# First attention of a two-layer trunk: the projections of the pair two ahead move from the turn's end to behind the next pair's transposes, and the raw values are kept in two places and copied by ScalarE

## The reference, cut to what matters

```python
def _mla_project(hn, pos, w_in, g_q, w_qup, g_kv, g_qn):
    ...
    q = (_rms_norm(c_q, g_q) @ w_qup).reshape(b, l, A_HEADS, A_DQK)
    q = _rms_norm(jnp.concatenate([q[..., :A_NOPE], _rope(q[..., A_NOPE:], pos)], axis=-1), g_qn)
    return q, _rms_norm(c_kv, g_kv), _rope(k_pe, pos)

def _mla_keys(latent, k_pe, w_kvup, g_kn):
    ...
    k = _rms_norm(jnp.concatenate([kv[..., :A_NOPE], k_pe_h], axis=-1), g_kn)
    return k, kv[..., A_NOPE:]
```

## Time and profile before

| what | us |
|---|---|
| median of 3 executions (lowest 2487.96, highest 2492.0) | 2488.02 |
| the profiled execution | 2487.95 |
| its span, first to last instruction | 2486.1 |
| TensorE busy in the span | 2292.0 (92%) |
| VectorE busy | 1729.8 (70%) |
| ScalarE busy | 1072.8 (43%) |
| GpSimd busy | 350.0 (14%) |
| the first attention's turns 0 to 5 | 521.52 to 767.79 |

### The profile page before, as it was taken

How to read it: one execution, slowest core, us unless ns; L and a number is a source line. 1 busy time by engine, 2 the same in 40 slices (tenths; PEclk the granted TensorE clock), 3 DMA queues, 4 the chain that set the end, 5 groups by cost and what they waited for, 6 DMA issues and landing times. The chain is left out here.

```text
span 2486.1 us, 45839 instructions
## 1 busy us (share of the span) xinstructions
PE 2292.0 (92%) x16594; PEld 2198.7 (88%) x16594; DVE 1729.8 (70%) x2714; ACT 1072.8 (43%) x1759; POOL 350.0 (14%) x300
## 2 busy tenths in 40 slices
PE   4999999588878989999999999999979989999997
PEld 4999999577877989999987899999867878999997
DVE  8976974456666599499535895795456657985973
ACT  5533532345555455145322552453236555542541
POOL 1000001134344100000114000001044321000001
PEclk9999999778988999999999999999978789999998
DMA  2222232000000222222213223223221212222221
GB/s 105 101 87 91 101 114 66 19 19 9 18 9 26 77 80 95 104 85 91 91 60 131 89 99 110 85 84 102 68 51 40 46 30 85 102 91 87 101 103 60
DMA packets 72794, 187.35 MB, mean 75 GB/s; under 512 B 40720, under 2 KB 42288, under 8 KB 61440
## 3 DMA queue, kind: packets, MB, share of 16 engines
q1 hardware_dynamic: 71424, 181.67, 21.7%
q0 software_dynamic: 1280, 4.49, 0.5%
HBM read 178.79 MB, written 7.35 MB: 75 GB/s over the span
## 5 line engine op out<-in xcount | busy, mean ns | idle before, releaser
L566 PE MATMUL ps<-xs_hi,w_hi 128*128 128x272 f32 x1408 | 411.6, 292 | 50.0 <-DVE w_lo_more L1515 28.3
L568 PE MATMUL ps<-xs_hi,w_lo 128*128 128x272 f32 x1408 | 409.4, 291 | 0.0
L567 PE MATMUL ps<-xs_lo,w_hi 128*128 128x272 f32 x1408 | 408.4, 290 | 0.0
L1038 ACT ACTIVATE w_hi<-raw 128x1408 fp32r<-128x1408 f32 (+3 forms) x124 | 145.9, 1183 | 507.1 <-PE ps L591 246.9
L1067 ACT ACTIVATE w_hi<-w_blocks 128x1024 fp32r<-128x1024 f32 x176 | 186.8, 1062 | 326.3 <-PE ps L568 160.5
L566 PEld LDWEIGHTS ps<-xs_hi,w_hi 128*128 128x128 f32 x1408 | 267.8, 190 | 53.9 <-issue 29.8
L566 PE MATMUL ps<-xs_hi,w_hi_more 128*128 128x272 f32 x1056 | 306.2, 290 | 1.2 <-ACT scratch L1113 0.9
L567 PE MATMUL ps<-xs_lo,w_hi_more 128*128 128x272 f32 x1056 | 305.7, 290 | 0.0
L591 PE MATMUL ps<-hid_hi,w_hi 128*128 128x272 f32 x1312 | 273.7, 290 | 9.1 <-DVE w_lo L1485 5.5
L591 PE MATMUL ps<-hid_hi,w_lo 128*128 128x272 f32 x1312 | 272.3, 289 | 0.0
L591 PE MATMUL ps<-hid_lo,w_hi 128*128 128x272 f32 x1312 | 272.3, 289 | 0.0
(11 more groups left out here) (249 smaller groups left out, 5259.7 us busy)
## 6 DMA issues: line engine op xcount, KB each, us to landing
w_blocks<-w_ffn_in SPq DMA_DIRECT2D x88, 1024.0 KB, 4.8
raw<-w_ffn_out SPq DMA_DIRECT2D x64, 704.0 KB, 4.1
raw<-w_b_kv SPq DMA_DIRECT2D x16, 512.0 KB, 3.6
raw<-w_a_out SPq DMA_DIRECT2D x8, 512.0 KB, 3.7
raw<-w_b_q SPq DMA_DIRECT2D x8, 512.0 KB, 3.6
raw<-w_b_out SPq DMA_DIRECT2D x8, 512.0 KB, 3.7
raw<-w_a_in SPq DMA_DIRECT2D x4, 672.0 KB, 4.0
raw<-w_a_qup SPq DMA_DIRECT2D x8, 288.0 KB, 2.8
```

What stands on the lines that cost most here:

```text
L566: pe.matmul(out, lhs[0], rhs[0], start=start, stop=False, skip_group_check=more)
L567: pe.matmul(out, lhs[0], rhs[1], start=False, stop=False, skip_group_check=more)
L568: return pe.matmul(out, lhs[1], rhs[0], start=False, stop=stop, skip_group_check=more)
L1038: act.activation(wh[par][:, 0:n], raw[par][:, 0:n], ACT.Copy).then_inc(w_hi, 1)
```

## The change

What it does, by engine:

- TensorE: `turn_staged` transposes the queries first, waiting for them alone ("qn"), then computes head 0's values (`between`), then waits for the keys and transposes them. `project_q` and `project_kv` of pair p + 2 come right behind, ahead of head 1's transposes; `w_uses` is reordered to match. Head 1's values now end the turn.
- ScalarE: the weight splits open the turn (in turn 6, `ahead`, the output projection's first unit). Behind the staging come `project(p + 2)`, which now copies both keys and raw values (L1307 of the changed kernel is the values' copy), and the squares of the keys.
- VectorE: the weight splits open the turn. Keys are normalised inside `stage`, behind the two query lows. `take_q` and `project` follow the staging; the five copies of raw values are gone. The sums of squares of the keys stand at the end of the turn, ahead of the output's low part.
- GpSimd: the queries of pair p + 2 between the two heads' normalisations, then the power for the keys, the staged values, the shared key part.
- The raw values of even pairs lie in the upper columns of `raw[0]` and `raw[1]` (`v_even`), those of odd pairs in `vr` (`v_odd`). The loop's body holds two turns, and runs three times. SP waits for GpSimd's staged values of pair 6 before it loads the output projection's units.

The arithmetic is the same. The core of the diff, first the tables, SP and TensorE:

```diff
 PROJ = {
     "pe": ["q0", "q1", "kv0", "kv1", "kv2", "kv3"],
-    "act": ["sqq", "k0", "k1", "k2", "k3", "k4", "sqk"],
...
+    "act": ["k0", "v0", "k1", "v1", "sqq", "k2", "v2", "k3", "v3", "k4", "v4", "sqk"],
+    "dve": ["q0", "q1", "q2", "rope_c", "rope_a", "rope_b", "rope", "ssq", "msq", "ssk", "ssk2", "ms", "kn"],
...
+        v_even = (raw[0][:, SLOT - 4 * 2 * DV:SLOT].rearrange("p (t g w) -> p t g w", t=4, g=2),
+                  raw[1][:, SLOT - NT * 2 * DV:SLOT].rearrange("p (t g w) -> p t g w", t=NT, g=2))
+        v_odd = (vrv[:, 0:4], vrv[:, 4:NK])
...
-            every += turned(1)
             if mla:
                 every += [(f"q{n}", p + 2, projects, [("proj", "dve", f"q{n}")]) for n in range(3)]
-                every += [(f"kv{n}", p + 2, projects, [("proj", "dve", f"v{n}")]) for n in range(5)]
+                every += [(f"kv{n}", p + 2, projects, [("proj", "act", f"v{n}")]) for n in range(5)]
+            every += turned(1)
...
+            sp.wait_ge(*M["stagev"]["pool"].at("v", PAIRS - 2))
             load_out(MO)
...
                     if mla:
-
-                        pe.wait_ge(*prj["pool"].at("kpe", it))
-                        pe.wait_ge(*prj["dve"].at("kn", it))
+                        pe.wait_ge(*prj["pool"].at("qn", it))
...
                     for name, v, t0 in (("tq", qsv, 0), ("tp", ksv, 0), ("tc", ksv, NT)):
+                        if mla and name == "tp":
+                            if between is not None:
+                                between()
+                            pe.wait_ge(*prj["pool"].at("kpe", it))
+                            pe.wait_ge(*prj["dve"].at("kn", it))
...
-                    if stages and not mla:
+                    if stages:
                         turn_staged(p + 1, uses, before, lambda: values(0, p))
                     else:
                         values(0, p)
-                        if stages:
-                            turn_staged(p + 1, uses, before)
+                    if mla and projects:
+                        project_q(p + 2, uses, before)
+                        project_kv(p + 2, uses, before)
...
                     values(1, p)
-                    if mla and projects:
-                        project_q(p + 2, uses, before)
-                        project_kv(p + 2, uses, before)
```

ScalarE:

```diff
-                def turn_of(p, stages, projects):
+                def turn_of(p, stages, projects, odd=False):
+                    if mla and projects:
+                        split_units(p + 2)
+                    elif mla and stages:
+                        ahead(U + 2 * PAIRS)
                     split_p(0, 0, p)
                     if not mla:
                         stage_values(p)
-                    elif stages:
-                        square_keys(p + 1)
...
                     if stages:
                         stage(p + 1)
-                        if mla and projects:
-                            split_units(p + 2)
-                        elif mla:
-
-                            ahead(U + 2 * PAIRS)
+                    if mla and projects:
+                        project(p + 2, odd)
+                        square_keys(p + 2)
```

VectorE:

```diff
+                        if mla and step == "q":
+                            norm_keys(it)
...
                 def turn_of(p, stages, projects):
+                    if mla and projects:
+                        split_units(p + 2)
+                    elif mla and stages:
+                        ahead(U + 2 * PAIRS)
                     for j in range(4):
                         top(1, j, p)
                         split_p(0, j, p)
-                        if j == 0 and mla and stages:
-                            mean_square_keys(p + 1)
...
                     if stages:
-                        if mla:
-                            norm_keys(p + 1)
                         stage(p + 1)
...
+                    if mla and projects:
+                        take_q(p + 2)
+                        project(p + 2)
...
+                    if mla and projects:
+                        mean_square_keys(p + 2)
                     dve.wait_ge(*att["act"].at("o", p))
```

GpSimd:

```diff
+                    if mla and projects:
+                        queries(p + 2)
                     if stages:
                         normalise(0, p + 1)
-                        if mla:
-                            stage_values(p + 1)
-                    if projects:
-                        step(p + 2)
+                    if mla:
+                        if projects:
+                            power_keys(p + 2)
+                        if stages:
+                            stage_values(p + 1, not odd)
+                        if projects:
+                            shared_keys(p + 2)
```

More of the change, by code:

```diff
@@ L829, in turn_staged @@
                             mm.then_inc(sem_, 1)
-                            if (name, g) == ("tp", 0) and between is not None:
+                            if not mla and (name, g) == ("tp", 0) and between is not None:
                                 between()
@@ L944, in attention @@
                     project_kv(1, first[1], first[0])
-                with pe.Fori(0, PAIRS - 2) as p:
-                    turn_of(p, True, True)
+                if mla:
+                    pe.wait_ge(*prj["act"].at("v4", 1))
+                    with pe.Fori(0, PAIRS // 2 - 1) as m:
+                        turn_of(2 * m, True, True)
+                        turn_of(2 * m + 1, True, True)
+                else:
+                    with pe.Fori(0, PAIRS - 2) as p:
+                        turn_of(p, True, True)
                 turn_of(PAIRS - 2, True, False)
@@ L1312, in stage_values @@
                     act.wait_ge(vpad, 2 if mla else 5)
-                    for src, dst in v_parts:
+                    for src, dst in zip(v_odd if odd else v_even, v_split):
                         act.activation(dst[0], src, ACT.Copy).then_inc(L["stagev"]["act"].sem, 1)
@@ L1386, in attention @@
                     split_units(1)
-                    project(1)
-                with act.Fori(0, PAIRS - 2) as p:
-                    turn_of(p, True, True)
-                turn_of(PAIRS - 2, True, False)
-                turn_of(PAIRS - 1, False, False)
+                    project(1, True)
+                    square_keys(1)
+                    with act.Fori(0, PAIRS // 2 - 1) as m:
+                        turn_of(2 * m, True, True, False)
+                        turn_of(2 * m + 1, True, True, True)
+                else:
+                    with act.Fori(0, PAIRS - 2) as p:
+                        turn_of(p, True, True)
+                turn_of(PAIRS - 2, True, False, False)
+                turn_of(PAIRS - 1, False, False, True)
             attention(M, True, gq, gk)
@@ L1923, in turn_of @@
                         low(hid[1][r, c], ps[r, 7, hh * DEC:(hh + 1) * DEC], hid[0][r, c], None, ainc)
-                    if mla and projects:
-                        take_q(p + 2)
-                        project(p + 2)
                 if mla:
@@ L1947, in attention @@
                     project(1)
-                with dve.Fori(0, PAIRS - 2) as p:
-                    turn_of(p, True, True)
+                    mean_square_keys(1)
+                    with dve.Fori(0, PAIRS // 2 - 1) as m:
+                        turn_of(2 * m, True, True)
+                        turn_of(2 * m + 1, True, True)
+                else:
+                    with dve.Fori(0, PAIRS - 2) as p:
+                        turn_of(p, True, True)
                 turn_of(PAIRS - 2, True, False)
@@ L2202, in stage_values, with project_at, turn_of @@
                                            ).then_inc(L["stagev"]["pool"].sem, 1)
-                def turn_of(p, stages, projects):
+                def project_at(it):
+                    queries(it)
+                    power_keys(it)
+                    shared_keys(it)
+                def turn_of(p, stages, projects, odd=False):
                     if not mla:
@@ L2225, in attention @@
                     meanwhile()
-                with pool.Fori(0, PAIRS - 2) as p:
-                    turn_of(p, True, True)
-                turn_of(PAIRS - 2, True, False)
-                turn_of(PAIRS - 1, False, False)
+                if mla:
+                    with pool.Fori(0, PAIRS // 2 - 1) as m:
+                        turn_of(2 * m, True, True, False)
+                        turn_of(2 * m + 1, True, True, True)
+                else:
+                    with pool.Fori(0, PAIRS - 2) as p:
+                        turn_of(p, True, True)
+                turn_of(PAIRS - 2, True, False, False)
+                turn_of(PAIRS - 1, False, False, True)
             add_squares(X0, ("sq0", "sq1"))
```

87 lines of the change are left out of this document (39 added, 48 removed).

## The result

The changed kernel takes 2498.65 us (median of 20 executions, 2489.74 to 2519.11) beside 2487.49 us (20 executions, 2482.07 to 2502.72) before: a ratio of 1.0048, 95% interval 1.0033 to 1.0062. It is slower, by 0.5%. The profiled execution took 2497.41 us, its span is 2495.6.

A forecast was written before the change was run, and what follows sets the result against it. In the first attention TensorE was taken to wait on a chain of ScalarE and VectorE, at a lowered clock. Six turns (+3), turn 6 (+8.5) and the first pair (-1.5) gave +10 on 2487.95: 2498 us, range 2484 to 2511.

The forecast's parts named there:

- Part 1: Turn's start, from T0 (end of second head's values) to last scores: splits and lows delay the fourth transposes, +0.65 us.
- Part 4: GpSimd's staged values beside VectorE's weight splits: each turn loses +0.5 us, bounds 0 and 0.9.
- Part 2: Last scores to the end of staging: queries and first head's values run first, -1.85 us a turn.
- Part 3: Projections, then second head: same work, ScalarE's extra copies cost 0 us, between -0.5 and +0.7.
- Part 5: Clock in turns 0 to 5: slower level falls on work behind two waits, +2.5 us a turn, bounds 0.9 and 3.4.
- Part 6: Turn 6: output weights' load waits for GpSimd's staged values and its split opens the turn, +8.5 us, bounds +7 and +10.
- Part 7: First pair, ahead of the turns: the 8 query transposes run earlier, in a wait, -1.5 us.
- Faster: Rival, chance 0.12: clock loss under 0.6 us a turn and no part 4, turns of 39.1, total 2482.5 us.
- Slower still: Rival, chance 0.20: slower clock on projections, or GpSimd and VectorE block each other fully; turns of 42.3, total 2504 us.
- Within the bound: Rival, chance 0.26: clock loss 1.5 and part 4 half, turns of 40.3, total 2490 us.
- The stall isn't there: Rival: no stall in turn 6, if weights were loaded before; its chance is part of the first two rivals'.

The follow-up runs named there:

- experiment 9: Changed kernel with the loop's weight splits at the turn's end and turn 6's first-unit split behind the staging, GpSimd's power still first: 2474.79 us.
- experiment 5: Kernel before with the staging order alone: queries transposed first, head 0's values between, keys normalised inside `stage`; projections stay at the turn's end: 2484.47 us.
- experiment 6: Kernel before with the new staging order and ScalarE copying the raw values, without the moved projections, splits and squares: 2480.86 us.
- experiment 4: Kernel before with only the raw values' copies moved from VectorE to ScalarE, nothing else moved: 2484.16 us.
- experiment 8: Changed kernel with only the loop's weight splits moved to the turn's end, a turn earlier; turn 6 and GpSimd's order unaltered: 2482.64 us.
- experiment 3: Changed kernel with turn 6's first-unit split behind the staging and GpSimd's staged values ahead of the power: 2481.61 us, run again 2481.07 us.
- experiment 2: Changed kernel with only GpSimd's order altered, staged values ahead of the power for the keys: 2490.08 us.
- experiment 1: Changed kernel with only turn 6's split of the output projection's first unit put back behind the staging: 2487.63 us.

## Why the prediction was right

The predicted 2498.0 us stands beside 2498.65. In turn 3, against the forecast without the clock (the clock there was 0.92):

| stretch | forecast | turn 3 |
|---|---|---|
| end of second values to last scores (parts 1, 4) | 7.04 + 0.65 + 0.5 = 8.19 | 9.24 |
| last scores to projections (part 2) | 11.36 - 1.85 = 9.51 | 10.32 |
| projections, second head (part 3) | 11.57 + 9.77 = 21.34 | 20.91 |
| turn | 39.04 | 40.47 |

**Part 1** held up to the splits: the output's lows end at T0 + 3.36 (forecast 3.36), ScalarE's splits at T0 + 3.7 (3.6). The fourth transposes start at T0 + 6.79; 5.6, and 6.1 with part 4, was the forecast.

**Part 4** is the term that was too small: 1.08 us (2.43 - 1.35), over the 0.5 that I took and over the upper bound of 0.9, and in turns 1 and 2 1.6 and 2.3 (in turn 0 nothing). The page of the Trainium skill that I weighed there, SBUF — State Buffer, section "SBUF: two separate sides", speaks of a lock for a whole instruction. The trace agrees with it here: the second split (1.75 instead of 0.68) waits for GpSimd's first value tile: at its 0.68 us it would have begun at 651.86, and the first of two value tiles, from 650.58 on, takes 1.42 us and ends at 652.0. The step that failed is "the rows show less than a full wait": the keys' 1.87 beside 1.36 was one overlap by chance, not the price of a full one.

**Part 2** gave 1.04 of the 1.85 beside turn 2, and 1.70 beside the mean of the six turns before (12.02): turn 2 was the shortest of turns 1 to 5 there, and in the other four the slower level, which I took to fall on transposes that wait anyway, cost 1.1 to 1.4 us. The keys' normalisation took 1.35 as forecast (1.36) and ended at +6.76 instead of +6.1. In turn 3 that delay is the clock's: the maximum of the last scores begins 1.71 us behind their start (657.68 - 655.97) instead of 1.06. In turn 4 of experiment 9, at a clock of 1.00, it begins at 1.07, but VectorE's scaling runs beside GpSimd there and takes 0.93 instead of the 0.56 that I took, and the stretch is 10.06. By itself this part can't be told from nothing in the whole time (experiment 5), with the copies it is part of a gain of 0.3% (experiment 6).

**Part 3** was 0.43 us better than zero, inside its bounds. Of the copies, experiment 4 shows no cost.

**Part 5** was too large, and made up for part 4. No turn of the changed kernel had a full clock, but one of experiment 9 did; windows of its turns 1 and 4, the same instructions:

```profile
561.10:602.30 41.20, 36.77 (x242) 33.99 (x241) 24.73 (x56) 21.90 (x55) 16.75 (x15) 0.83 0.05 15
677.80:715.20 37.40, 30.75 (x241) 28.34 (x240) 25.30 (x57) 21.88 (x55) 17.10 (x14) 1.00 0.05 15
```

37.4 us at 1.00, and 39.07 on average over its six turns: the clock cost 1.7 us a turn. With the longer wait of the changed kernel (4.14 instead of 1.81) a turn at full clock would be about 39.7, an estimate, and its mean turn is 41.39: again 1.7, not 2.5. The clean turn was forecast 0.7 too short and the clock 0.8 too dear; 41.55 against 41.39 is right by two errors of opposite sign, and the range, not the point, is what the working had earned.

**Part 6** was right step by step. From the turn's start at 768.10: power ends at +3.9 (forecast 3.8), values at +6.6 (6.6), load issued at +6.62 (6.6), ScalarE's split starts at +10.3 (10.5), VectorE's ends at +12.65 (12.7), fourth transposes at +13.7 (13.6). The turn grew by 9.35 us (8.5).

**Part 7** seems to come out (-1.75, forecast -1.5), but isn't shown by it: experiment 4, which doesn't have this part, starts its turns at 519.4 us, and experiment 8, which does, at 521.8; and the kernel of experiment 3, profiled twice, starts them at 519.87 and at 521.70. **Not forecast:** turn 7, whose work did not change, is 1.8 us longer, at a clock of 0.72 instead of 0.82 (below).

**The rivals.** "Faster" asked for a clock loss under 0.6 us a turn: it was 1.7. "Slower still" asked for a full block of the two engines, and had that; but its price for the clock, 2.9 us, was not paid (its own sum is 1 us too high: 8 and the 7 of parts 6 and 7 are +15, not +16). "Within the bound" had nearly the clock (1.5 beside 1.7), but asked for half of part 4, and it was double. "The stall isn't there" fell with 11.07 us of wait.

## What to carry to other kernels

Work moved off one engine's path has to land in another engine's idle time, and the order inside the receiving turn decides that: the splits cost 10 to 16 us more where they opened the turn, ahead of what TensorE waits for, than where VectorE waited anyway. When a buffer gets a second use, follow the load that now waits for the last reader, and take whatever waits for that load off the front of every engine's queue. A stretch that got shorter is not yet a shorter turn: compare every stretch, over all turns and with the granted clock beside it, before you call a saving made or missed. The staging order saved 1.7 us a turn, and the same instructions behind it took 1.6 longer.

## What the runs showed of the hardware

**VectorE and GpSimd side by side.** The two splits of a pair's weights (128x576 and 128x512) take 1.35 us alone and 2.43 beside GpSimd's staged values; these take 2.80 or 2.79 without the splits and 3.36 beside them. Together they lose 1.08 + 0.56 = 1.6 us in one place of a turn. Only an instruction that starts while the other engine's runs was slow (splits 0.76, then 1.75), so where the two begin, by tenths of a microsecond, sets the price. In turn 2 the first split starts as GpSimd's second value tile runs and takes 2.10 us, GpSimd's key part then starts under that split and takes 1.68 (1.15 alone), and the second split starts under the key part and takes 1.64: 3.66 for the pair, while the values, which came first, took 2.76. The power is different. In experiment 2 the first split (1.03 us) starts at 646.38, some 0.3 ahead of the values' end, and takes 0.3 longer; the power starts at 646.75 under it and takes 0.5 longer; but the second split, wholly beside the power, takes 0.70, as alone. So the lock for a whole instruction, which the Trainium skill speaks of (SBUF — State Buffer, section "SBUF: two separate sides"), is not what the trace shows for the power: by it either the second split would have waited some 3 us, or the power for both splits, to 648.03, 1.3 us in place of 0.5.

**The same instructions at different clocks.** Turn 7 holds the same instructions in every kernel. Its windows in the kernel with both faults mended (experiment 3), and in the one with the splits moved but the stall of turn 6 in place:

```profile
793.50:813.50 20.00, 14.40 (x93) 12.66 (x92) 9.33 (x25) 10.38 (x27) 5.67 (x6) 0.91 0.00 0
```
```profile
797.90:819.10 21.20, 15.52 (x92) 13.62 (x92) 9.34 (x25) 10.42 (x27) 5.67 (x6) 0.84 0.00 0
```

20.0 us at 0.91, 21.2 at 0.84, 21.5 at 0.82 (before), 23.3 at 0.72 (changed): a tenth of clock is worth some 1.7 us of 20. Which of these it gets is not shown to be the stall's doing: the kernel of experiment 9, without a stall, took 23.25, and that of experiment 3, profiled twice, took 20.00 and 21.57. So a single profile can be off by some microseconds in the first attention for no reason that lies in the edit: the loop took 241.03 and 248.33 us with the same instructions in experiment 1 and in the changed kernel.
